# Expert weights read in 16 KB pieces, tokens in that order, and one turn for two experts

## The reference

```python
def grouped_moe(x, router_w, router_bias, w_gate, w_up, w_down):
    x2 = x.reshape(-1, d)                                  # 256 x 1024
    aff = sigmoid(x2 @ router_w)                           # 16 experts
    # best of 4 groups, then the best 2 of its 4 experts; gates = their aff, normalised
    def step(acc, ew):
        g_e, wg_e, wu_e, wd_e = ew                         # 1024x512, 1024x512, 512x1024
        h = silu(x2 @ wg_e) * (x2 @ wu_e)
        return acc + (h @ wd_e) * g_e[:, None], None
```

## Time and profile before

| | |
|---|---|
| median of 3 runs (lowest to highest) | 1563.94 us (1562.49 to 1570.64) |
| the profiled execution, its span | 1561.53 us, 1559.8 us |
| PE, DVE, ACT, POOL busy | 1399.9 (90%), 428.5 (27%), 272.6 (17%), 61.5 (4%) us |
| DMA | 307.75 MB, mean 197 GB/s over the span |
| experts stage 0 (first product to end of last scatter) | 206.3 to 456.5 us |
| experts stage 1 | 687.7 to 939.8 us |

### The profile page before, as it was taken

How to read it: one execution, slowest core, us unless ns; L and a number is a source line. 1 busy time by engine, 2 the same in 40 slices (tenths; PEclk the granted TensorE clock), 3 DMA queues, 4 the chain that set the end, 5 groups by cost and what they waited for, 6 DMA issues and landing times.

```text
span 1559.8 us, 15911 instructions
## 1 busy us (share of the span) xinstructions
PE 1399.9 (90%) x6338; PEld 903.6 (58%) x6338; DVE 428.5 (27%) x961; ACT 272.6 (17%) x598; POOL 61.5 (4%) x97
## 2 busy tenths in 40 slices
PE   7868689999979996869999997999889996999997
PEld 6654444454435774445444535876667685888743
DVE  1992311111130232221111103145522304222201
ACT  4022110010010333111000112131143403000000
POOL 4910000000000000000000000000000000000000
PEclk9979789999989995879999998998999998999999
DMA  9710259999995051329999995131223033344420
GB/s 361 230 48 18 96 201 395 396 393 393 393 393 176 0 179 65 108 74 393 393 395 396 393 393 202 54 109 54 76 86 108 1 108 108 109 161 162 162 81 27
DMA packets 146506, 307.75 MB, mean 197 GB/s; under 512 B 5634, under 2 KB 29950, under 8 KB 146447
## 3 DMA queue, kind: packets, MB, share of 16 engines
q1 hardware_dynamic: 139968, 298.85, 52.4%
q10 hardware_dynamic: 6479, 8.07, 1.6%
HBM read 305.86 MB, written 1.06 MB: 197 GB/s over the span
## 4 chain that ended last, share of the span: by engine, by line
PE 81%; DVE 11%; DMA 5%; issue 2%; ACT 1%; ACTq 0%; DVEq 0%; POOL 0%; POOLq 0%
PE psum L233 35%; PE psum L1289 13%; PE psum L1325 6%; PE psum L544 6%; PE psum L2512 5%; DMA ring<-in_moe_w_up 5%; DVE arena L878 3%; PE psum L1336 3%; PE psum L759 2%; PE psum L733 2%; PE psum L1310 2%; PE psum L425 1%; PE psum L1474 1%; PE psum L1472 1%; PE psum L2170 1%
## 5 line engine op out<-in xcount | busy, mean ns | idle before, releaser
L233 PE MATMUL psum<-xT,ring 128*128 128x256 f32 (+2 forms) x1792 | 405.4, 388 | 6.2 <-POOLq L405 5.2
L233 PEld LDWEIGHTS psum<-xT,ring 128*128 128x128 f32 x1792 | 341.4, 192 | 66.5 <-issue 11.0
L1289 PE MATMUL psum<-ring,arena 128*64 128x512 f32 x1024 | 226.2, 594 | 3.2 <-issue 1.7
L1289 PEld LDWEIGHTS psum<-ring,arena 128*64 128x64 f32 x1024 | 73.9, 137 | 138.5 <-issue 138.2
L1325 PE MATMUL psum<-ring,arena 128*64 128x512 f32 x512 | 117.7, 614 | 1.8 <-ACT arena L1250 1.8
L233 PE MATMUL psum<-arena,x_nat 128*128 128x128 f32 x512 | 69.1, 292 | 16.7 <-issue 16.7
L233 PEld LDWEIGHTS psum<-arena,x_nat 128*128 128x128 f32 x512 | 63.5, 202 | 29.1 <-issue 28.2
L1325 PEld LDWEIGHTS psum<-ring,arena 128*64 128x64 f32 x512 | 36.9, 141 | 70.5 <-issue 68.8
L1180 DVE TENSOR_TENSOR arena<-psum,arena 64x512 f32<-64x512 f32 x32 | 22.3, 695 | 200.1 <-ACT arena L1236 200.1
L2512 PE MATMUL psum<-ring,arena 128*128 128x512 f32 x176 | 75.7, 592 | 0.0
L878 DVE SCALAR_TENSOR_TENSOR arena<-arena,vec 128x256 f32<-128x256 f32 x150 | 75.0, 575 | 0.7
(11 more groups left out here) (302 smaller groups left out, 1308.5 us busy)
## 6 DMA issues: line engine op xcount, KB each, us to landing
ring<-in_moe_w_gate SPq DMA_DIRECT2D x32, 2048.0 KB, 15.8
ring<-in_moe_w_up SPq DMA_DIRECT2D x32, 2048.0 KB, 19.7
ring<-in_moe_w_down SPq DMA_DIRECT2D x32, 2048.0 KB, 15.7
ring<-in_w_in SPq DMA_DIRECT2D x11, 2048.0 KB, 15.3
ring<-in_w_up SPq DMA_DIRECT2D x22, 1024.0 KB, 7.7
ring<-in_a_w_pw SPq DMA_DIRECT2D x6, 2048.0 KB, 19.5
ring<-in_w_down SPq DMA_DIRECT2D x5, 2048.0 KB, 7.7
ring<-in_w_kv SPq DMA_DIRECT2D x4, 2048.0 KB, 19.4
```

The lines of the kernel that those rows point to most:

```text
L233: last = nc.tensor.matmul(dst, lhsT, rhs, start=(n == 0), stop=(n == len(pairs) - 1))
L1289: last = pe.matmul(bank(j)[part, :], tokens[:, k, side * SEATS:side * SEATS + SEATS], slot_k(u + n)[:, k, :], start=(k == 0), stop=(k == K ...
```

## The change

Weights: every expert matrix is now read so that partition p holds the rows p * 8 to p * 8 + 7 (gate, up) or p * 4 to p * 4 + 3 (down), 16 KB that lie in one piece in memory. For this the tokens must come in the same order: the routing stage copies x_nat with a step of 8 features into by_row, the gather reads by_row, and x_nat itself is scaled by ALPHA in place (base is gone). The product of SiLU and up is written in the order that the down matrix needs, with a step of 4 elements in its sources.

Turn: expert 0 puts its hidden rows into partitions 0 to 63 and expert 1 into 64 to 127 of one tile, for which gate and up swap halves for expert 0. Four full transposes turn both, in place of eight products of 64 x 128.

Gates: a second matrix, gated, is the one-hot matrix times the gates; it is transposed in place of seats, and the outputs are copied without scaling. The four small products are gone. gatedT has two buffers.

Order of a pair on TensorE: GU0, S, GU1, scatter of the pair before, T, X0, X1, Y0 and Y1. All pairs are written out; there are no hardware loops.

```diff
-IN_PAIR = ... ("GU0", "S", "GU1", "X0", "T", "X1", "Y0", "Y1")
+IN_PAIR = ... ("GU0", "S", "GU1", "T", "X0", "X1", "Y0", "Y1")
...
         def load_expert(u, kind, layer, e):
-            ... src.rearrange("(k p) n -> p k n" ...
+            src = a[f"moe_w_{kind}"][layer, e].rearrange("(p k) n -> p k n", p=P)
+            load(u, src, slot_k(u, D) if kind == "down" else slot_k(u))
...
-            act.activation(base[:, :, :], x_nat[:, 1:3, :], ACT.Copy, scale=ALPHA)
+            for t in range(2):
+                act_step(act.activation(by_row[:, t, :, :], x_nat[:, t + 1, :].rearrange("p (f k) -> p k f", k=KC),
+                                        ACT.Copy))
+            act.activation(x_nat[:, 1:3, :], x_nat[:, 1:3, :], ACT.Copy, scale=ALPHA)
...
-                            [(x_nat[:, t + 1, k * P:k * P + P], sources[:, t, :]) for t in range(2)])
+                            [(by_row[:, t, k, :], sources[:, t, :]) for t in range(2)])
...
+            def gate_seats(p):
+                for t in range(2):
+                    for side in range(2):
+                        e = 2 * p + side
+                        ins = dve.tensor_scalar(gated[:, t, side * SEATS:side * SEATS + SEATS], counting[:, 0:SEATS],
+                                                slot_of[:, t, e:e + 1], gates[:, t, e:e + 1], ALU.is_equal, ALU.mult)
+                ins.then_inc(gated_ready, 1)
...
-                dve.tensor_tensor(hid[HIGH, side, :], bank(j)[HIGH, :], silu_g[HIGH, side, :], ...
+                by_row = lambda x: x.rearrange("s (f k) -> s k f", k=DE // P)
+                dve.tensor_tensor(hid_both[part, :].rearrange("s (k f) -> s k f", f=P), by_row(bank(j)[part, :]),
+                                  by_row(silu_g[part, 0, :]), ALU.mult).then_inc(bank_free[j % BANKS], 1)
...
-                dve.tensor_copy(gate_col[LOW], bank(j)[LOW, 2 * P:2 * P + 1])
-                dve.tensor_copy(gate_col[HIGH], bank(j)[HIGH, 2 * P + 1:2 * P + 2])
-                dve.tensor_copy(seatsT, bank(j)[:, 0:2 * P]).then_inc(bank_free[j % BANKS], 1)
+                dve.tensor_copy(gatedT[:, p % 2, :], bank(j)[:, 0:2 * P]).then_inc(bank_free[j % BANKS], 1)
...
             def turn_seats(p):
                 for t in range(2):
-                    pe.transpose(bank(j)[:, t * P:t * P + P], seats[:, t, :], ident[:, :])
-                products(bank(j)[:, 2 * P:2 * P + 2], [(seats[:, t, :], gate_cell[:, t, :]) for t in range(2)]
-                         ).then_inc(job_done, 1)
+                    last = pe.transpose(bank(j)[:, t * P:t * P + P], gated[:, t, :], ident[:, :])
+                last.then_inc(job_done, 1)
...
             def turn(p):
-                for side in range(2):
-                    for k in range(DE // P):
-                        at = (4 * side + k) * SEATS
-                        last = pe.matmul(bank(j)[:, at:at + SEATS], hid[HIGH, side, k * P:k * P + P],
-                                         ident[HIGH, HIGH], start=True, stop=True)
+                for k in range(DE // P):
+                    last = pe.transpose(bank(j)[:, k * P:k * P + P], hid_both[:, k * P:k * P + P], ident[:, :])
...
+            for p in range(PAIRS_E):
+                for j in gathers(p):
+                    read_out(pe, j)
+                gate_up(0, p)
+                turn_seats(p)
+                gate_up(1, p)
+                if p == 1:
+                    pe.wait_ge(cleared, 1)
+                if p > 0:
+                    scatter(p - 1)
+                turn(p)
+                if p < LAST:
+                    fetch(0, p + 1)
+                    fetch(1, p + 1)
+                down(p)
             scatter(LAST)
```

More of the change, by code:

```diff
@@ L364, in _ @@
             src = units[u][0]
[L365 to L372, removed]
             if u == 1:
@@ L1128, in body @@
                             for half in range(2):
[L1129 removed]
+                                part = x_nat[:, t + 1, half * 512:half * 512 + 512]
                                 ins = dve.tensor_tensor(part, part, psum[:, 4 + 2 * t + half, :], ALU.add)
@@ L1163, in _, with seat @@
         def _(dve):
[L1164 to L1169, removed]
+            def seat(p):
                 for t in range(2):
                     for side in range(2):
+                        e = 2 * p + side
@@ L1194, in gathered, with summed @@
+            def gathered(j):
+                job_ready(dve, j)
                 dve.tensor_copy(tokens[:, 4:8, :], bank(j).rearrange("p (c s) -> p c s", c=4)).then_inc(
                     bank_free[j % BANKS], 1)
-            def summed(p, i=0):
+            def summed(p):
                 j = job("Y1", p)
[L1199 to L1212, removed]
+                job_ready(dve, j)
+                dve.tensor_copy(y_pair[:, 512:D], bank(j)).then_inc(bank_free[j % BANKS], 1)
@@ L1214, in _ @@
             seat(0)
+            gate_seats(0)
             gathered(B + 1)
             dve.memset(psum[:, BANKS:2 * BANKS, :], 0.0).then_inc(cleared, 1)
[L1218 to L1221, removed]
+            for p in range(PAIRS_E):
+                if p < LAST:
+                    seat(p + 1)
+                hidden(0, p)
+                turned_seats(p)
+                hidden(1, p)
+                if p < LAST:
+                    gate_seats(p + 1)
+                    gathered(job("X1", p))
+                summed(p)
@@ L1258, in _ @@
[L1258 to L1262, removed]
+            gathered(B)
+            for p in range(PAIRS_E):
+                silu(0, p)
+                silu(1, p)
+                j = job("T", p)
+                job_ready(act, j)
+                act.activation(hidT_both, bank(j).rearrange("p (k s) -> p k s", s=P), ACT.Copy).then_inc(
+                    bank_free[j % BANKS], 1)
+                if p < LAST:
+                    gathered(job("X0", p))
+                j = job("Y0", p)
+                job_ready(act, j)
+                act.activation(y_pair[:, 0:512], bank(j), ACT.Copy).then_inc(bank_free[j % BANKS], 1)
@@ L1264, in _, with free, fetch @@
         @block.tensor
         def _(pe):
[L1266 to L1273, removed]
+            def free(j):
+                pe.wait_ge(bank_free[j % BANKS], j // BANKS)
+            def fetch(half, p):
                 j = gathers(p)[half]
-                pe.wait_ge(seats_ready, p + 1 + i)
-                free(j, i)
+                pe.wait_ge(seats_ready, p + 1)
+                free(j)
@@ L1323, in down @@
                     for k in range(DE // P):
                         for side, part in enumerate((LOW, HIGH)):
-                            last = pe.matmul(bank(j)[part, :], hidT[:, side, k * SEATS:k * SEATS + SEATS],
+                            last = pe.matmul(bank(j)[part, :], hidT_both[:, k, side * SEATS:side * SEATS + SEATS],
                                              slot_k(u + side, D)[:, k, half * 512:half * 512 + 512], start=(k == 0),
@@ L1328, in down, with scatter @@
                     last.then_inc(job_done, 1)
-            def scatter(p, i=0):
-                read_out(pe, job("Y0", p), i)
-                read_out(pe, job("Y1", p), i)
+            def scatter(p):
+                read_out(pe, job("S", p))
+                read_out(pe, job("Y0", p))
+                read_out(pe, job("Y1", p))
                 for t in range(2):
                     for half in range(2):
-                        last = pe.matmul(psum[:, BANKS + 2 * t + half, :], seatsT[:, t * P:t * P + P],
+                        last = pe.matmul(psum[:, BANKS + 2 * t + half, :], gatedT[:, p % 2, t * P:t * P + P],
                                          y_pair[:, half * 512:half * 512 + 512], start=False, stop=(p == LAST),
@@ L1341, in scatter @@
                             last.then_inc(scattered, 1)
-                if p < LAST:
-                    last.then_inc(scattered, 1)
-            def pair(p, i=0):
-                for j in gathers(p):
-                    read_out(pe, j, i)
-                gate_up(0, p, i)
-                if p > 0:
-                    scatter(p - 1, i)
-                turn_seats(p, i)
-                gate_up(1, p, i)
-                if p < LAST:
-                    fetch(0, p + 1, i)
-                turn(p, i)
-                if p < LAST:
-                    fetch(1, p + 1, i)
-                down(p, i)
             fetch(0, 0)
             fetch(1, 0)
-            pair(0)
-            pe.wait_ge(cleared, 1)
-            with pe.Fori(0, LAST - 1) as i:
-                pair(1, i)
-            pair(LAST)
+            for p in range(PAIRS_E):
+                for j in gathers(p):
[8 more added lines that the diff above has]
+                turn(p)
+                if p < LAST:
+                    fetch(0, p + 1)
+                    fetch(1, p + 1)
+                down(p)
             scatter(LAST)
```

109 lines of the change are left out of this document (45 added, 64 removed).

## The result

| | before | changed |
|---|---|---|
| median (lowest to highest), 4 runs each | 1564.84 us (1562.49 to 1570.64) | 1524.33 us (1523.13 to 1528.58) |
| profiled execution, span | 1561.53, 1559.8 us | 1523.13, 1521.4 us |

The ratio is 0.9749, 95% interval 0.9727 to 0.977. The change makes the kernel 2.5% faster; 1528 (1519 to 1545) was forecast.

What follows compares the result with a forecast made beforehand. TensorE was taken to bound the expert stages, with DMA just behind; savings of 23.8 + 6.9 + 3 + 1.6 + 0 = 35.3 us from 1561.5, plus 2.4 us to the median, gave 1528 us, range 1519 to 1545.

Steps and rivals of the forecast that it cites:

- Turn 23.8 us, seat job 6.9 us: On TensorE, over 16 pairs: four transposes for the turn save 1.49 us each, dropping four small seat matmuls 0.43 us each.
- DMA at 429 GB/s, waits gone (1.6 us): Expert weights in 16 KB pieces load at an estimated 429 GB/s, so TensorE's three weight waits, 1.6 us in sum, go.
- the lead of 5.5 us: Weight ring starts full in each expert stage, hiding about 5.5 us of DMA lag over the seven refilled pairs.
- The threshold of 422: Weight DMA in expert stages: below 422 GB/s the ring's lead is used up, each GB/s costing 0.5 us a stage.
- Clock in the last pair 3 of 4.3 us: Last pair's down job: with the first idle gone, 3 us of the 4.3 us lost to low TensorE clock come back.
- Idle ends cancel: Moving the scatter saves 1.58 us of idle in each stage's last pair and adds 1.58 us in its first.
- The copies hidden: Routing stage: ScalarE's two strided token copies finish no later than VectorE's chain; price 0, at most 0.5 us a stage.
- The entry to a stage left as it is: Before each expert stage's first gather, TensorE's 7.8 us idle after the preceding stage was taken as unchanged.
- Rival A: Weight DMA rate stops at 410 GB/s, costing 6.0 us a stage: 1540 us; chance 0.12.
- B: Weight pieces not merged or no faster than 395 GB/s, costing 14.3 us a stage: 1557 us; chance 0.06.
- C: 16 KB weight pieces load slower, at 234 GB/s, costing 168 us a stage: 1864 us; chance 0.04.
- D: Unrolled code arrives late in the expert stages, stopping each pair once for 3 us, 42 us: 1570 us; chance 0.04.

Runs made afterwards that it cites:

- e1: Kernel before with only the 16 KB weight pieces, their token order and the strided product: 1564.88 us, ratio 0.9993 to the kernel before.
- e2: Changed kernel with weights read in pieces as before, 2 KB (gate, up) and 4 KB (down): 1562.42 us, ratio 0.9979 to the kernel before.
- e5: Changed kernel measured again, with nothing altered, on another chip: 1529.24 us, ratio 0.9758 to the kernel before.
- e6: Changed kernel, half the gather before the first pair's turn, last pair's scatter taking both first halves before the second down output is read out: 1516.8 us, ratio 0.9683.
- e8: Changed kernel with the previous pair's scatter put ahead of the seat job in each stage's last pair: 1526.95 us, ratio 0.9744 to the kernel before.
- e4: Changed kernel with the old turn, eight products of 64 x 128 a pair in place of four transposes: 1559.42 us, ratio 0.9968 to the kernel before.
- e9: Kernel before with its hardware loops written out on all engines and the SyncE queue, nothing else: 1557.66 us, ratio 0.996 to the kernel before.
- e3: Changed kernel with all expert weights in pieces of 4 KB: 1542.22 us, ratio 0.9851 to the kernel before.

## Why the prediction was right

- *TensorE bounds, and its savings count only if the DMA keeps up.* Shown: e1 and e2 gain at most 0.4% each, both together 2.4% (e5).
- *Turn 23.8 us, seat job 6.9 us.* Together 1.92 us a pair, measured 2.06 (30.98 to 28.92). The turn gave its 1.49 us. The seat job gave 0.28 in place of 0.43 (271.15 to the next product at 271.52), and the gather, which I had at nothing, 0.29: 3.67 us in one piece against 3.96 around the narrow products. More than half of that comes from no longer being cut in two: in the first pairs of e6, where it stands around the four full transposes, it takes 1.96 + 1.88 = 3.84.
- *DMA at 429 GB/s, waits gone (1.6 us).* The rate was 426, and the waits became 2.4 us instead of none (1.4 in e5); the lead of 5.5 us, read from a kernel whose deficit was small, was somewhat too large. In e2 each stage loses 16.7 us up to the end of its last wait, in waits and in slower jobs between them; (32.0 - 28.9) x 7 = 21.7 us of lag less that leave 4 to 5, since pairs lie 31.9 to 32.0 apart. The threshold of 422 was thus nearer 425. Of e2's miss (28 expected, 34 measured) this is 2.4 us; 1.7 is the clock, which fell once more behind the last wait of the first stage, and 1.0 that e5 itself waits less than was taken.
- *Clock in the last pair 3 of 4.3 us.* All of it came back (8.57 and 9.92 to 7.09). My reason, that the first idle goes, was one of two that the runs bear out: e8 opened the idle again and the clock stayed. The Trainium skill's sentence on transposes ("TensorE: Matmul & The Clock Gate", Part 4) would have let the clock fall there; that did not happen, neither in the last pair nor behind the 1.86 us in the first. In e2 the clock did fall in five of eight pairs where the two transposes of the seat job and a wait of 2.2 to 2.9 us came one after the other; no run here tells how much of that is the transposes'. That the first pair was at risk, as the prediction said, e4 shows: with the narrow turn the clock falls there.
- *Idle ends cancel.* Nearly: +1.86 us in the first pair, -1.58 in the last, 0.6 us more in both stages. The strided product costs 1.07 in place of 0.70 us, inside the bound of 0.7.
- *The sum.* 35.3 us were added up and the experts stages gave 35.6. That it fits so well is partly luck. Against the sum, the seat job gave 2.4 us less, the waits 2.4 and the idle ends 0.6; the gather gave 4.1 us more (14 of 0.29) and the clock 1.3.
- *The copies hidden.* The two strided copies took 2.06 us each and ScalarE ended at 190.4, 1.7 us before VectorE's chain. Right.
- *HBM side as the limit.* The rows at 426 GB/s contradict the figure of about 358 in the Trainium skill ("DMA: Bandwidth & Descriptors", Bandwidth) on this core as those of before did.
- *The entry to a stage left as it is.* Not so: the second one became 4.9 us shorter, the first 2.1 longer (its idle 9.14 us, and a gather of 6.70 us), and e5 repeats only the second. e9 shows the second with no other part of the change. It is why the profiled execution gained 38.4 us and not 35.3.
- Rival A's step lies at e3, B's at e2, where both came within 6 us of the times given for them. C did not happen (the rate rose with the piece up to 16 KB), nor did D (e9).

## What to carry to other kernels

Where a ring of buffers hides a DMA that is a few per cent slower than the compute, work out both paces per turn and the lead of the ring: a saving on one side alone is worth little more than that lead. The rate by piece size can be taken from the kernel's own trace as a fixed time a piece plus a time a KB, and held four times beyond its last point here. When a reordering covers a wait in the steady state, look at the first and last turn: here 1.2% of the stages was still to be had there.

## What the runs showed of the hardware that was not expected

- Narrow products (64 rows, 64 columns) between wide ones cost their neighbours a little as well: behind them the gather takes 3.77 us (e4), behind full transposes 3.67. Cut in two, it takes 3.96 around narrow products (before) and 3.84 around full transposes (e6).
- TensorE's clock fell behind an idle of 1.6 to 1.9 us and 2 us of narrow products, with a second idle of 0.9 us behind them (before, e1 and e9, to 0.51 in before) or none (first pairs of e4, 0.50); idles as long around four full transposes left it at 1.00. Of eight waits of 2.2 to 2.9 us behind two transposes (e2) five brought it down and three did not.
- Ahead of the first gather of the second stage, TensorE idles 8.8 to 8.9 us in before, e1 and e4 and 3.1 to 3.4 us in the other kernels; why is open. Stages with the same code differ by up to 5 us (attention) and 8 us (all behind the second experts stage) between the profiles, and by 2.6 and 4.3 us between the two of the changed kernel. In this kernel, differences below half a per cent have to be read stage by stage.
